# Decode attention: where the spread queries are copied, and the order of turn and values on TensorE

## The chip, the cores and the metric

One NeuronCore of a Trainium2 chip runs the whole program, two decoder layers in one launch. The metric is the time of one execution on the device in microseconds (us); less is better. The engines are TensorE (PE; its weight loads are PEld), VectorE (DVE), ScalarE (ACT), GpSimd (POOL) and SyncE (SP), which only issues transfers. Each engine works its own list of instructions in order, and they meet only at semaphores.

## The reference, cut to what matters

The program computes two layers of a hybrid decoder for a prompt of 1024 tokens and for 8 decode samples of 4 tokens. What the change touches is the attention of the decode samples to their paged cache of 4096 past positions. Each position has 128 latent values and 32 rotary values, which all 8 heads share:

```python
ckv_past = cache_ckv[l][page_table].reshape(DB, past_len, KV_LORA)      # 8 samples x 4096 x 128
kpe_past = cache_kpe[l][page_table].reshape(DB, past_len, ROPE_DIM)     # 8 samples x 4096 x 32
...
s = (jnp.einsum('bthc,blc->bhtl', ql, kc) + jnp.einsum('bthr,blr->bhtl', qp, kr)).astype(jnp.float32) * MLA_SCALE
p = jax.nn.softmax(s, axis=-1).astype(kc.dtype)
return jnp.einsum('bhtl,blc->bthc', p, kc)
```

A sample has 32 query rows (8 heads x 4 tokens). Everything is float32. The same layer holds a gated linear attention (GLA) with a state per sample, whose stage ends just ahead of this one.

## The kernel before, in words

A layer is a row of stages that end in barriers (`stage_end`): every compute engine drains, adds one to `stage_done` and waits for the others. Stage 3 is the GLA; stage 4 is the decode attention, and the change lies in stage 4 and at the end of stage 3.

**Stage 4, one iteration per sample n = 0 to 7.** `cache_load(n)` on GpSimd issues two indirect gathers by page number, of the latent rows (2 MB, into one of four buffers `ck`) and of the rotary rows (0.5 MB, into one of two buffers `kr_c`). DVE turns the keys in five pieces (`turn_keys`, 32x32 block transposes, 128 x 1024): piece 0 is the rotary part, pieces 1 to 4 are 32 latent columns each. The turned piece lies in one of three buffers `ct`. TensorE multiplies each piece with the queries (`scores(n, b)`, 32 matmuls of 64 rows x 256 columns in the records), adding up over the five pieces in PSUM. Then DVE takes the maximum (`maxima`), ACT the exponential (`probs`), TensorE turns the probabilities (`turn_probs`, 8 transposes), ACT copies them to SBUF (`take_probs`), and TensorE multiplies them with the latent rows (`values`, 64 matmuls); ACT keeps the result (`keep_o`). DVE takes the maximum of sample n-1 between its pieces 2 and 3 of sample n.

**The queries.** `q_dec` holds the latent queries with the latent index on the partitions. For piece b, `scores` wants the 32 rows 32(b-1) to 32b of it on all four groups of 32 partitions, since the keys of four groups are turned at a time: `q8[b]`. So `spread_q(b)` copies 32 rows of `q_dec` to four places, and the rest of `q8[b]` is zero. Before the change SP issues these as transfers from SBUF to SBUF: for b = 1, 2 early in stage 3, for b = 3, 4 when `g_zero` is 2. GpSimd gives that mark after two memsets that stand behind `cache_load(1)` in stage 4, and `cache_load(1)` waits until the GLA's states are stored (`states_stored`), because the buffer of gather 1 lies over them. `q8[0]` is written by DVE in stage 2.

**The order on TensorE in stage 4 before the change.** For each n: `scores(n, 0)`, then `values(n-2)` from n = 2 on, then pieces 1 to 3, then `turn_probs(n-1)`, then piece 4. Sample 0 has the scores against the new tokens (`new_scores`) behind its piece 4, 33 matmuls, and DVE takes their maxima (`new_maxima`) before it turns the first keys of sample 1. Gather n waits for the first turned piece of sample n-2 (the rotary buffer is free) and, from n = 4 on, for `pv_done` of sample n-4 (the latent buffer is free).

**At the end of stage 3** DVE makes the operands of the decode samples' GLA (line 2307 gives `g_dve`), TensorE works with them, and the last DVE operations (line 2330) update the eight states. GpSimd has nothing left there after `cache_load(0)`.

**The wait of the change, as it stands in `scores`:**

```python
pe.wait_ge(ct_ready, m + 1)
if n == 0 and b >= 1:
    pe.wait_ge(kr_or_q_moved, 48 + 16 * (8 if b <= 2 else 16))
if b == 0 and n >= 2:
    pe.wait_ge(pd_ready, n)
```

Of the kernel before, what the change touches and what calls it, by code (L numbers as in the profile page):

```python
# [24 lines left out]
P = 128  # L25
DEPTH, D, SEQ, DB, DT = 2, 1024, 1024, 8, 4
KT = D // P
ND = DB * DT
# [5 lines left out]
H, NOPE, ROPE, VD = 8, 64, 32, 64  # L34
# [9 lines left out]
KROW = 32  # L44
BLK = PAST // P
# [14 lines left out]
STEPS = P // KROW + 1  # L60
NCT = 3
# [117 lines left out]
def build(nc, ins, outs):  # L179

    with ExitStack() as ctx:
# [32 lines left out]
        def view(at, *shape):  # L214
            n = int(np.prod(shape))
            v = arena[:, at:at + n]
            names = [f"a{k}" for k in range(len(shape))]
            if len(shape) == 1:
                return v
            return v.rearrange(f"p ({' '.join(names)}) -> p {' '.join(names)}",  # L220
                               **{n_: s for n_, s in zip(names[1:], shape[1:])})
# [37 lines left out]
        q_dec = view(SC, DB, ND)  # L259
        q8 = [view(at, DB, 2, ND) for at in (SC + 2560, SC + 1536, SC + 2048, SC + 4096, SC + 4608)]  # L260
        S2 = SC + 3072
        qswap = [view(S2, TOK), view(SC + 4896, TOK)]
        row_sum, row_rec = view(SC + 1024, 2, 2, NT), view(SC + 1056, 2, 2, NT)
# [28 lines left out]

        ck = [view(at, BLK, P) for at in (XN, XN + 5120, XN + 9216, XN + 13312)]
        kr_c = [view(at, BLK, ROPE) for at in (XN + 4096, XN + 20480)]
        ct = view(XN + 17408, NCT, BLK, KROW)
        pd, pdt = view(SC + 320, 8, P), view(S2, 2, 512)
        o_part = [view(at, P) for at in (SC + 1344, *(SC + 5120 + P * n for n in range(6)), XN + 512)]
        w_sel, o_lat, pn_t = view(XN, DB, ND), view(XN + 256, H, DB, DT), view(XN + 640, 2, ND)
        ckv_rep = view(S2, 4, ND)
        m_all, l_all, m_neg = (view(SC + 256 + DB * k, DB) for k in range(3))  # L300
        m_new, l_new = view(SC + 280, DB), view(SC + 288, DB)
        spare = rope.rearrange("p a n -> p (a n)")
# [206 lines left out]
        def _(sp):  # L509
# [20 lines left out]
            for l in range(DEPTH):  # L530
# [73 lines left out]
                def spread_q(b):  # L604

                    for a in range(4):
                        sp.dma_start(q8[b][KROW * a:KROW * (a + 1), :, a % 2, :], q_dec[KROW * (b - 1):KROW * b]).then_inc(kr_or_q_moved, 16)

# [12 lines left out]
                for h in range(GH):  # L621
                    rows, cols = slice(GK * h, GK * (h + 1)), slice(GV * h, GV * (h + 1))
                    sp.dma_start(outs["gla_s"][bass.ds(l, 1), :, h].rearrange("a b k v -> (a k) b v"), d_state[rows, :, cols]).then_inc(states_stored, 16)
                sp.wait_ge(g_zero, 2)
                for b in (3, 4):
                    spread_q(b)
                sp.wait_ge(stage_done, 4 * (BARRIERS.index(4) + 1))
# [146 lines left out]
        def _(pe):  # L774
# [33 lines left out]
            for l in range(DEPTH):  # L808
# [354 lines left out]
                def new_scores():  # L1163

                    pe.wait_ge(tail_dve, 1)
                    pe.transpose(ps[:, 0, 256:256 + P], ckv_rep.rearrange("p r k -> p (r k)"), ident).then_inc(tail_pe, 1)
                    for n in range(DB):
                        out = ps[0:ND, 0, n * ND:(n + 1) * ND]
                        pe.matmul(out, q_dec[:, n, :], ckv_new, start=True, stop=False)
                        mm = pe.matmul(out, q8[0][64:96, n, 0, :], kr_new[64:96, :], start=False, stop=True)  # L1170
                    mm.then_inc(tail_pe, 1)
# [7 lines left out]
                def scores(n, b):  # L1179

                    m = STEPS * n + b
                    pe.wait_ge(ct_ready, m + 1)
                    if n == 0 and b >= 1:
                        pe.wait_ge(kr_or_q_moved, 48 + 16 * (8 if b <= 2 else 16))
                    if b == 0 and n >= 2:
                        pe.wait_ge(pd_ready, n)
                    for x in range(2):
                        for g in range(4):
                            for h in range(2):
                                r = slice(64 * h, 64 * (h + 1))  # L1190
                                mm = pe.matmul(ps[ND * g:ND * (g + 1), 4 + 2 * (n % 2) + h, 256 * x:256 * (x + 1)], q8[b][r, n, x, :],  # L1191
                                               ct[r, m % NCT, 8 * g:8 * (g + 1), :], start=b + x == 0, stop=b == STEPS - 1, skip_group_check=True)
                    mm.then_inc(sc_done if b == STEPS - 1 else ct_used, 1)
# [24 lines left out]
                for n in range(DB):  # L1218
                    scores(n, 0)
                    if n >= 2:  # L1220
                        values(n - 2)
                    for b in range(1, 4):
                        scores(n, b)
                    if n >= 1:
                        turn_probs(n - 1)
                    scores(n, 4)
                    if n == 0:
                        new_scores()

                values(DB - 2)  # L1230
                pe.wait_ge(tail_dve, 3)
# [751 lines left out]
        def _(dve):  # L1983
# [36 lines left out]
            for l in range(DEPTH):  # L2020
# [125 lines left out]
                def q_pe(i, e):  # L2146

                    h = 2 * i + e
                    dve.wait_ge(q_rope, 4 * i + 1 + e)
                    src = q_h[64:96, 2 * (i % 2) + e, SEQ:TOK].rearrange("p (b t) -> p b t", b=DB)  # L2150
                    for j in range(4):
                        step.mark(dve.tensor_copy(q8[0][32 * j:32 * j + 32, :, j % 2, DT * h:DT * (h + 1)], src))

# [582 lines left out]
        def _(pool):  # L2736
# [29 lines left out]
            for l in range(DEPTH):  # L2766
# [6 lines left out]
                pool.wait_ge(vg_done, NT + 1)  # L2773
                step(pool.memset(q8[0], 0.0))

# [17 lines left out]
                step(pool.memset(d_state, 0.0))  # L2793
                step.mark(pool.memset(q8[1], 0.0))
                step(pool.memset(q8[2], 0.0))
                pool.memset(g_k, 0.0).then_inc(g_zero, 1)
# [22 lines left out]
                def cache_load(n):  # L2819

                    for dst, cache in ((ck[n % NSLOT], "cache_ckv"), (kr_c[n % 2], "cache_kpe")):
                        pool.indirect_dma_start(dst.rearrange("p j c -> p (j c)"), None,
                                                ins[cache].rearrange("l n (q k) c -> (l n q) (k c)", k=KROW),
                                                bass.IndirectOffsetOnAxis(ap=page_i[:, n:n + 1], axis=0)).then_inc(ck_full[n % NSLOT], 16)

                pool.wait_ge(at_done, NT)
                cache_load(0)
                step.restart()
                stage_end(pool, 3)


                for n in range(1, DB):
                    if n == 1:
                        pool.wait_ge(states_stored, 16 * (DB + 4 + 2 * GH))
                    if n >= 2:
                        pool.wait_ge(ct_ready, STEPS * (n - 2) + 1)
                    if n >= NSLOT:
                        pool.wait_ge(pv_done, n - NSLOT + 1)
                    cache_load(n)
                    if n == 1:  # L2840
                        step.mark(pool.memset(q8[3], 0.0))
                        step.sync()
                        pool.memset(q8[4], 0.0).then_inc(g_zero, 1)
                for j in range(NSLOT):
# [190 lines left out]
```

## Time and profile before

| | |
|---|---|
| median of 3 runs | 2570.68 us (2569.37 to 2576.91) |
| the profiled execution | 2552.38 us, span 2550.6 us |
| mean granted TensorE clock of the profiled execution | 0.965 |
| busy: TensorE / weight loads / DVE / ACT / GpSimd | 92% / 54% / 46% / 26% / 19% |
| stage 4, layer one | 516.0 to 636.0 us |
| stage 4, layer two | 1789.2 to 1904.5 us |

The profile is of one execution. The timeline lists runs of instructions of one kind with their start, their length, their line and count, and in brackets the idle time of the engine ahead of them and what ended it; "issue" is a wait for nothing that the profile shows. PE in the windows is TensorE; PEclk is the granted clock, where 1.00 is 2.4 GHz and 0.50 is 1.2 GHz.

### The profile page before, as it was taken

The page shows a single profiled execution, that of the slowest core. Times are in us where ns is not written, and L with a number is a line of the kernel's source. Part 1 is how long each engine was busy: PE and PEld are TensorE (multiplying, and loading weights), DVE is VectorE, ACT ScalarE, POOL GpSimd, SP SyncE. Part 2 cuts the span into 40 slices and gives each one's busy share as a digit, 9 for nine tenths or more (in the row PEclk, how much of TensorE's full clock was granted, in tenths as well). Part 3 has the DMA queues.
Part 4 walks back from the last instruction along what each step waited for, and adds up shares of the span by engine and source line. Part 5 has one row for each costly group of instructions (what it writes and reads, how often), then busy time and mean ns, then how long its engine had stood idle before and what let it go on. Part 6 is the DMA issues. An engine that isn't in the chain of part 4 may idle for free.

```text
span 2550.6 us, 41562 instructions
## 1 busy us (share of the span) xinstructions
PE 2336.2 (92%) x17636; PEld 1385.2 (54%) x17636; DVE 1166.7 (46%) x2074; ACT 653.9 (26%) x1404; POOL 472.5 (19%) x574
## 2 busy tenths in 40 slices
PE   8999998869999999999899999988699999999994
PEld 5645556646666765333366455566466676733332
DVE  2365556855231344333253555568542332633324
ACT  1033444412111331111130334444121022311113
POOL 6003323410100001111260033234100000011113
PEclk9999999978999999999999999999799999999997
DMA  5001001153233128999830010011521421599996
GB/s 190 11 19 30 11 12 42 43 182 119 98 127 120 70 111 323 399 423 423 337 137 11 20 30 11 11 42 43 212 106 55 153 75 66 211 355 409 424 418 255
DMA packets 88224, 391.35 MB, mean 153 GB/s; under 512 B 29390, under 2 KB 33100, under 8 KB 68524
## 3 DMA queue, kind: packets, MB, share of 16 engines
q1 hardware_dynamic: 69884, 309.91, 31.9%
q0 software_dynamic: 17568, 76.57, 7.8%
q8 instruction: 143, 2.34, 0.4%
q10 hardware_dynamic: 576, 2.10, 0.2%
q14 instruction: 53, 0.43, 0.1%
HBM read 355.31 MB, written 41.41 MB: 156 GB/s over the span
## 4 chain that ended last, share of the span: by engine, by line
PE 73%; DVE 11%; issue 4%; ACT 3%; DMA 3%; PEld 2%; POOL 1%; SPq 1%; POOLq 1%; PEldq 0%; DVEq 0%; ACTq 0%
PE ps L1483 12%; PE ps L802 8%; PE ps L825 8%; PE ps L1507 6%; PE ps L1391 5%; PE ps L893 4%; PE ps L973 4%; PE ps L1191 3%; PE ps L985 2%; DVE arena L2224 2%; PE ps L1001 2%; PEld ps L825 2%; PE ps L951 2%; PE ps L1469 2%; DMA arena<-yrow 1%
## 5 line engine op out<-in xcount | busy, mean ns | idle before, releaser
L1483 PE MATMUL ps<-arena 128*32 128x512 f32 x2304 | 317.0, 602 | 21.9 <-issue 16.2
L825 PE MATMUL ps<-arena,ring 128*128 128x352 f32 x936 | 279.9, 462 | 1.0 <-ACTq L487 1.0
L802 PE MATMUL ps<-x,ring 128*128 128x352 f32 x768 | 230.9, 462 | 11.9 <-DMA x<-in_x 10.4
L825 PEld LDWEIGHTS ps<-arena,ring 128*128 128x128 f32 x936 | 178.8, 191 | 100.2 <-issue 1.5
L2655 DVE COPY arena<-ps 128x1024 f32<-128x1024 f32 x44 | 53.9, 1225 | 336.3 <-PE ps L1469 336.3
L802 PEld LDWEIGHTS ps<-x,ring 128*128 128x128 f32 x768 | 146.5, 191 | 93.7 <-issue 13.6
L1483 PEld LDWEIGHTS ps<-arena 128*32 128x32 f32 x2304 | 92.9, 111 | 185.9 <-issue 185.9
L1507 PE MATMUL ps<-arena 128*32 128x512 f32 x1408 | 160.2, 595 | 3.8 <-ACT arena L1900 3.8
L2863 POOL DMA_INDIRECT arena<-xrow,arena x46 | 46.8, 1017 | 590.0 <-DVE arena L2630 319.4
L973 PE MATMUL ps<-arena 96*128 96x512 f32 (+3 forms) x384 | 144.9, 487 | 0.0
L1191 PE MATMUL ps<-arena 64*32 64x256 f32 x2560 | 94.9, 434 | 47.6 <-DMA arena<-arena 31.0
L1391 PE MATMUL ps<-arena,ring 128*128 128x352 f32 x384 | 117.7, 463 | 1.6 <-DVE arena L2488 1.6
L1669 ACT ACTIVATE ring<-ps 128x512 f32<-128x512 f32 (+2 forms) x192 | 87.1, 490 | 120.0 <-PE ps L985 120.0
L893 PE MATMUL ps<-arena,x 128*128 128x512 f32 x256 | 114.6, 608 | 2.2 <-ACT arena L1617 2.2
L1483 PE MATMUL ps<-ring,arena 128*32 128x512 f32 x512 | 116.0, 607 | 0.0
L985 PE MATMUL ps<-consts,ring 128*128 128x128 f32 x576 | 88.5, 280 | 22.2 <-ACT ring L1674 9.1
L1674 ACT ACTIVATE ring<-ps,nmax 128x128 f32<-128x128 f32 (+7 forms) x128 | 94.5, 740 | 52.9 <-DVE nmax L2127 52.4
L2358 DVE STREAM_TRANSPOSE arena<-arena 128x1024 f32<-128x1024 f32 x80 | 95.9, 1227 | 21.5 <-PE ps L1191 17.3
L2125 DVE TENSOR_TENSOR ps<-ps,consts 128x128 f32<-128x128 f32 x128 | 38.3, 299 | 143.8 <-PE ps L973 142.9
L1895 ACT ACTIVATE arena<-ps 128x256 f32<-128x256 f32 x44 | 16.9, 383 | 328.6 <-PE ps L1483 328.6
L2126 DVE TENSOR_REDUCE nmax<-ps 128x1 f32<-128x128 f32 (+7 forms) x128 | 97.0, 758 | 4.4
L1391 PEld LDWEIGHTS ps<-arena,ring 128*128 128x128 f32 x384 | 71.7, 190 | 46.1 <-issue 6.8
(470 smaller groups left out, 3705.1 us busy)
## 6 DMA issues: line engine op xcount, KB each, us to landing
arena<-in_w_gu SPq DMA_DIRECT2D x52, 2048.0 KB, 14.0
arena<-in_w_dn SPq DMA_DIRECT2D x64, 1024.0 KB, 11.9
ring<-in_ring SPq DMA_DIRECT2D x56, 512.0 KB, 3.7
ring<-in_w_gu SPq DMA_DIRECT2D x12, 2048.0 KB, 13.3
arena<-yrow SPq DMA_DIRECT2D x16, 1024.0 KB, 9.4
arena<-in_mem_k SPq DMA_DIRECT2D x16, 512.0 KB, 7.2
arena<-in_mem_v SPq DMA_DIRECT2D x16, 512.0 KB, 9.2
xrow<-arena SPq DMA_DIRECT2D x16, 512.0 KB, 8.6
```

The source lines that it names most:

```text
L802: mm = pe.matmul(ps[:, PIECE_BANKS[n % len(PIECE_BANKS)], 0:CH], ring[:, j % RING, k, :], x[:, k, tok], start=k == 0, stop=k == KT - 1)
L825: mm = pe.matmul(ps[:, (j % 2) * NCH + c, 0:CH], ring[:, j // per, (j % per) * units + k, :], src[:, k, tok], start=k == k0, stop=k == uni ...
L893: mm = pe.matmul(ps[:, 6 + t % 2, :], x[:, k, t * P:t * P + m], wvg[:, k, :], start=k == 0, stop=k == KT - 1)
L973: mm = pe.matmul(ps[:, bank + at // 512, 0:end - at], q_h[0:QK, b, qb * P:(qb + 1) * P], k_h[0:QK, b, at:end], start=True, stop=True)
L985: mm = pe.transpose(ps[:, bank, (kb % 4) * P:(kb % 4 + 1) * P], prob[:, e, kb * P:(kb + 1) * P], ident)
L1191: mm = pe.matmul(ps[ND * g:ND * (g + 1), 4 + 2 * (n % 2) + h, 256 * x:256 * (x + 1)], q8[b][r, n, x, :], ct[r, m % NCT, 8 * g:8 * (g + 1), ...
L1391: mm = pe.matmul(ps[:, (j % 2) * NCH + c, 0:CH], ring[:, slot, (j % 2) * XH + k, :], co[:, k, tok], start=k == 0, stop=k == XH - 1)
L1483: mm = pe.matmul(ps[r, 2 + n % 2, :], xb_t[:, n % 2, k, r], w_gu[e % NW][:, k, :], start=k == 0, stop=k == KT - 1, skip_group_check=True)
L1507: mm = pe.matmul(ps[r, 4 + f, :], h_t[:, k, r], w_dn[e % NW][:, k, f * 512:(f + 1) * 512], start=k == 0, stop=k == 1, skip_group_check=True)
L1674: act.activation(prob[:, e, 0:w], ps[:, 2 * e:2 * e + 2, :].rearrange("p a n -> p (a n)")[:, 0:w], ACT.Exp, bias=nmax[:, e, 1:2], scale=ML ...
L2126: step(dve.reduce_max(nmax[:, e, 0:1], sc, AX))
L2358: dve.transpose(ct[:, m % NCT], keys).then_inc(ct_ready, 1)
```

## The change

The spread queries of pieces 3 and 4 are copied by GpSimd at the end of stage 3, behind `cache_load(0)`, and not by SP; `cache_load(1)` is issued right behind them, ahead of the barrier. For this, buffers are placed anew so that neither the copies nor gather 1 lie over anything that the GLA still needs: `q8` becomes two halves per piece, gather 1's latent buffer moves off the states, and `ct`, `pd`, `o_part`, `ckv_rep` and the maxima move. Gather 2 is now the one that waits for `states_stored`. On TensorE `turn_probs(n-1)` stands behind piece 2 of sample n, and `values(n-1)` behind piece 4. No matmul, no gather and no DVE or ACT operation is added or removed; SP loses eight transfers a layer, and GpSimd gets eight copies.

```diff
-        q8 = [view(at, DB, 2, ND) for at in (SC + 2560, SC + 1536, SC + 2048, SC + 4096, SC + 4608)]
         S2 = SC + 3072
+        Q8 = (SC + 2560, SC + 1536, SC + 2048, S2 + 1280)
+        q8 = [[view(at + DB * ND * x, DB, ND) for x in range(2)] for at in Q8]
+        q8.append([view(at, DB, ND) for at in (S2 + 2592, SC + 1280)])
...
-        ck = [view(at, BLK, P) for at in (XN, XN + 5120, XN + 9216, XN + 13312)]
-        kr_c = [view(at, BLK, ROPE) for at in (XN + 4096, XN + 20480)]
-        ct = view(XN + 17408, NCT, BLK, KROW)
+        ck = [view(at, BLK, P) for at in (XN, XN + 13312, XN + 5120, XN + 9216)]
+        kr_c = [view(at, BLK, ROPE) for at in (XN + 4096, XN + 17408)]
+        ct = view(XN + 18432, NCT, BLK, KROW)
...
 # SP
-                sp.wait_ge(g_zero, 2)
-                for b in (3, 4):
-                    spread_q(b)
...
 # TensorE, scores
-                    if n == 0 and b >= 1:
-                        pe.wait_ge(kr_or_q_moved, 48 + 16 * (8 if b <= 2 else 16))
+                    if n == 0 and b == 1:
+                        pe.wait_ge(kr_or_q_moved, 48 + 16 * 8)
+                    if n == 0 and b == 3:
+                        pe.wait_ge(g_zero, 2)
...
 # TensorE, the loop
                 for n in range(DB):
-                    scores(n, 0)
-                    if n >= 2:
-                        values(n - 2)
-                    for b in range(1, 4):
+                    for b in range(3):
                         scores(n, b)
                     if n >= 1:
                         turn_probs(n - 1)
-                    scores(n, 4)
-                    if n == 0:
+                    for b in range(3, STEPS):
+                        scores(n, b)
+                    if n >= 1:
+                        values(n - 1)
+                    else:
                         new_scores()
 
-                values(DB - 2)
...
 # GpSimd
+                def spread_q(b):
+
+                    for a in range(4):
+                        last = pool.tensor_copy(q8[b][a % 2][KROW * a:KROW * (a + 1)], q_dec[KROW * (b - 1):KROW * b])
+                        if a < 3:
+                            step.mark(last)
+                    return last
+
                 pool.wait_ge(at_done, NT)
                 cache_load(0)
+                pool.wait_ge(g_dve, 1)
+                step.mark(pool.memset(view(Q8[3], 2 * DB, ND), 0.0))
+                step.mark(pool.memset(q8[4][0], 0.0))
+                step(pool.memset(q8[4][1], 0.0))
+                pool.wait_ge(ck_full[0], 32)
+                step.mark(spread_q(3))
+                spread_q(4).then_inc(g_zero, 1)
+                pool.wait_ge(g_zero, 2)
+                cache_load(1)
                 step.restart()
                 stage_end(pool, 3)
 
 
-                for n in range(1, DB):
-                    if n == 1:
+                for n in range(2, DB):
+                    if n == 2:
                         pool.wait_ge(states_stored, 16 * (DB + 4 + 2 * GH))
                     if n >= 2:
                         pool.wait_ge(ct_ready, STEPS * (n - 2) + 1)
                     if n >= NSLOT:
                         pool.wait_ge(pv_done, n - NSLOT + 1)
                     cache_load(n)
-                    if n == 1:
-                        step.mark(pool.memset(q8[3], 0.0))
-                        step.sync()
-                        pool.memset(q8[4], 0.0).then_inc(g_zero, 1)
```

## Rows read from the trace of the kernel before

**Rows 1.** The page: busy times, and the group of line 1191.

```profile
PE 2336.2 (92%) x17636; PEld 1385.2 (54%) x17636; DVE 1166.7 (46%) x2074; ACT 653.9 (26%) x1404; POOL 472.5 (19%) x574
...
L1191 PE MATMUL ps<-arena 64*32 64x256 f32 x2560 | 94.9, 434 | 47.6 <-DMA arena<-arena 31.0
```

**Rows 2.** Timeline of TensorE at the start of stage 4, layers one and two.

```profile
517.42 5.38 PE L1191 MATMUL ps<-arena 64*32 64x256 f32 x96 [2.48 <-DVE arena L2358]
538.33 3.67 PE L1191 MATMUL ps<-arena 64*32 64x256 f32 x64 [15.53 <-DMA arena<-arena]
...
548.21 6.24 PE L1191 MATMUL ps<-arena 64*32 64x256 f32 x128 [2.75 <-DVE arena L2358]
...
1811.51 3.67 PE L1191 MATMUL ps<-arena 64*32 64x256 f32 x64 [15.47 <-DMA arena<-arena]
```

**Rows 3.** Timeline of GpSimd and SP, start of stage 4, layer one.

```profile
519.84 0.94 POOL L2822 DMA_INDIRECT arena<-in_cache_ckv,page_i  x1 [29.86 <-DMA out_gla_s<-arena]
...
523.17 10.71 SPq L607 DMA_DIRECT2D arena<-arena  x8
```

**Rows 4.** GpSimd's groups by line and shape: busy us, mean ns, idle before.

```profile
L2779 POOL TENSOR_TENSOR arena<-arena,rope 32x512 f32<-32x512 f32 x16 | 20.1, 1258 | 1.3 <-DMA arena<-arena 1.3
...
L2859 POOL TENSOR_TENSOR arena<-arena,consts 128x256 f32<-128x256 f32 x8 | 5.8, 724 | 319.3 <-DVE arena L2441 319.3
...
L2843 POOL MEMSET arena<- 128x512 f32 x2 | 1.0, 524 | 0.1
```

**Rows 5.** Timeline of stage 3's end, and line 2822's time from issue to landing.

```profile
489.04 0.95 POOL L2822 DMA_INDIRECT arena<-in_cache_kpe,page_i  x1 [0.30 <-issue]
...
500.66 0.49 DVE L2307 TENSOR_TENSOR arena<-arena 128x128 f32<-128x128 f32 x2
...
DMA to landing us min/median/max: 8.6/9.1/12.4
```

**Rows 6.** Timeline of DVE, first keys of sample 0.

```profile
516.03 4.69 DVE L2358 STREAM_TRANSPOSE arena<-arena 128x1024 f32<-128x1024 f32 x4
```

**Rows 7.** Windows: length, then busy us and count of each engine, PEclk, DMA.

```profile
519.00:520.00 1.00, 1.00 (x27) 0.56 (x19) 1.00 (x2) 0.00 (x0) 0.16 (x1) 0.50 0.00 0
...
523.00:526.00 3.00, 0.00 (x0) 0.00 (x0) 0.00 (x0) 0.00 (x0) 2.02 (x3) 1.00 1.01 421
...
543.20:545.50 2.30, 2.27 (x26) 1.66 (x25) 0.00 (x0) 0.00 (x0) 0.00 (x0) 1.00 0.00 0
```

**Rows 8.** Timeline around the exponentials of sample 2, layer one.

```profile
564.12 1.96 PE L1191 MATMUL ps<-arena 64*32 64x256 f32 x64
566.00 1.50 PE L1213 MATMUL ps<-arena 128*32 128x128 f32 x42
...
565.32 1.25 DVE L2358 STREAM_TRANSPOSE arena<-arena 128x1024 f32<-128x1024 f32 x1 [0.41 <-PE ps L1191]
...
568.91 0.19 ACT L1784 ACTIVATION_READ_ACCUMULATOR arena<-ps,arena 128x1 f32 x1
```

**Rows 9.** Timeline of TensorE in the loop: turns of both layers, a break.

```profile
563.09 1.09 PE L1202 MATMUL ps<-consts,arena 128*128 128x128 f32 x8
...
609.41 1.09 PE L1202 MATMUL ps<-consts,arena 128*128 128x128 f32 x8
...
1835.13 1.09 PE L1202 MATMUL ps<-consts,arena 128*128 128x128 f32 x8
...
1849.29 1.29 PE L1213 MATMUL ps<-arena 128*32 128x128 f32 x37 [0.99 <-issue]
...
1872.25 1.09 PE L1202 MATMUL ps<-consts,arena 128*128 128x128 f32 x8
...
1879.80 1.09 PE L1202 MATMUL ps<-consts,arena 128*128 128x128 f32 x8
```

**Rows 10.** GpSimd beside DVE in stage 3: timeline, and a group of the lines.

```profile
479.26 0.42 DVE L2241 TENSOR_TENSOR arena<-arena 128x256 f32<-128x256 f32 x1
479.35 0.51 POOL L2808 TENSOR_TENSOR arena<-arena 128x64 f32<-128x64 f32 x1 [2.00 <-ACT arena L1716]
...
L2808 POOL TENSOR_TENSOR arena<-arena 128x64 f32<-128x64 f32 x112 | 36.4, 325 | 27.8 <-ACT arena L1716 27.7
```

More of the change, by code:

```diff
@@ L290, in build @@
         d_q0, d_q = view(PR + 192, GH, ND), view(PR + 320, 2, GH, ND)
-        ck = [view(at, BLK, P) for at in (XN, XN + 5120, XN + 9216, XN + 13312)]
-        kr_c = [view(at, BLK, ROPE) for at in (XN + 4096, XN + 20480)]
-        ct = view(XN + 17408, NCT, BLK, KROW)
-        pd, pdt = view(SC + 320, 8, P), view(S2, 2, 512)
-        o_part = [view(at, P) for at in (SC + 1344, *(SC + 5120 + P * n for n in range(6)), XN + 512)]
+        ck = [view(at, BLK, P) for at in (XN, XN + 13312, XN + 5120, XN + 9216)]
+        kr_c = [view(at, BLK, ROPE) for at in (XN + 4096, XN + 17408)]
+        ct = view(XN + 18432, NCT, BLK, KROW)
+        pd, pdt = view(SC + 256, 8, P), view(S2, 2, 512)
+        o_part = [view(at, P) for at in (*(S2 + 1792 + P * n for n in range(6)), XN + 768, XN + 896)]
         w_sel, o_lat, pn_t = view(XN, DB, ND), view(XN + 256, H, DB, DT), view(XN + 640, 2, ND)
-        ckv_rep = view(S2, 4, ND)
-        m_all, l_all, m_neg = (view(SC + 256 + DB * k, DB) for k in range(3))
-        m_new, l_new = view(SC + 280, DB), view(SC + 288, DB)
+        ckv_rep = view(S2 + 1024, 4, ND)
+        m_all, l_all, m_neg = (view(S2 + 1152 + DB * k, DB) for k in range(3))
+        m_new, l_new = view(S2 + 1176, DB), view(S2 + 1184, DB)
         spare = rope.rearrange("p a n -> p (a n)")
@@ L1169, in new_scores @@
                         pe.matmul(out, q_dec[:, n, :], ckv_new, start=True, stop=False)
-                        mm = pe.matmul(out, q8[0][64:96, n, 0, :], kr_new[64:96, :], start=False, stop=True)
+                        mm = pe.matmul(out, q8[0][0][64:96, n, :], kr_new[64:96, :], start=False, stop=True)
                     mm.then_inc(tail_pe, 1)
@@ L1190, in scores @@
                                 r = slice(64 * h, 64 * (h + 1))
-                                mm = pe.matmul(ps[ND * g:ND * (g + 1), 4 + 2 * (n % 2) + h, 256 * x:256 * (x + 1)], q8[b][r, n, x, :],
+                                mm = pe.matmul(ps[ND * g:ND * (g + 1), 4 + 2 * (n % 2) + h, 256 * x:256 * (x + 1)], q8[b][x][r, n, :],
                                                ct[r, m % NCT, 8 * g:8 * (g + 1), :], start=b + x == 0, stop=b == STEPS - 1, skip_group_check=True)
@@ L2151, in q_pe @@
                     for j in range(4):
[L2152 removed]
+                        step.mark(dve.tensor_copy(q8[0][j % 2][32 * j:32 * j + 32, :, DT * h:DT * (h + 1)], src))
                 def inverse(i, hf):
@@ L2773, in _ @@
                 pool.wait_ge(vg_done, NT + 1)
-                step(pool.memset(q8[0], 0.0))
+                step(pool.memset(view(Q8[0], 2 * DB, ND), 0.0))
                 def rope_q(h, hf, cols):
@@ L2793, in _ @@
                 step(pool.memset(d_state, 0.0))
-                step.mark(pool.memset(q8[1], 0.0))
-                step(pool.memset(q8[2], 0.0))
+                step(pool.memset(view(Q8[1], 4 * DB, ND), 0.0))
                 pool.memset(g_k, 0.0).then_inc(g_zero, 1)
```

2 lines of the change are left out of this document (1 added, 1 removed).

## The prediction

> **What bounds the kernel now.** I read the page first, then the PE rows of the timeline in the decode attention stage, then what DVE, SP and GpSimd did in the same stretch, and last the clock windows. The page [rows 1] shows TensorE busy for 92% of the span, so only time in which TensorE stands still, or runs at the lower clock, is worth anything. One of its lines speaks of this change: the scores of line 1191 were held for 47.6 us, and 31.0 of it ended with a transfer from SBUF to SBUF.
>
> The timeline says where [rows 2]. In each layer TensorE does the first three score pieces of sample 0, stands for 15.5 us, does the other two and the new scores, stands 2.75 us, and goes into the loop over samples 1 to 7. The 15.5 us are the copies of the spread queries for pieces 3 and 4: SP issues eight transfers one after the other from 523.17, which takes 10.71 us, and the last lands at 538.3 [rows 3]. SP waited there for two memsets of GpSimd, which stood behind the issue of gather 1, and that behind a wait of 29.86 us for the stores of the states. 2 x 15.5 is the 31.0 of the page.
>
> **The spread copies.** What goes: eight SP transfers and the wait for them. What comes: before the barrier that ends the gated-linear stage GpSimd does three memsets (512, 256 and 256 columns), eight copies of 32 partitions x 256, and the two issues of gather 1. The trace has no copy of that form, nor any GpSimd operation that reads one group of partitions and writes another. The nearest rows [rows 4]: a memset of 512 columns takes 0.52 us, so 0.27 us for 256 is the lower end; a two-input operation on 128 x 256 takes 0.72, and on 32 x 512 1.26 us, the upper end. A copy reads one tensor and writes one, so I take 0.45, between the memset and the two-input operation of its width. Eight are 2.2 to 10.1 us, taken as 3.6.
>
> When: the copies wait for g_dve, which DVE's last multiply at line 2307 gives at 501.15, and for gather 0, whose second half was issued at 489.04 and with the longest landing of 12.4 us is there by 501.4 [rows 5]. Memsets from 501.2 to 502.3, copies to 505.9 (504.5 to 512.4), gather 1 issued in 2.5 us (twice 0.94 [rows 3] and two gaps of 0.3), so GpSimd is done at 508.4 (507.0 to 514.9). The barrier falls when DVE ends, just ahead of its first key transpose at 516.0 [rows 6]. GpSimd was idle all this time; even the upper end is hidden by 1 us. If that cover is gone, every us more of GpSimd is a us more per layer.
>
> With the queries there, piece 3 needs only its turned keys, and DVE had turned them at 520.7 (four transposes from 516.03 in 4.69 us [rows 6]). So it starts when piece 2 ends, at 522.8. **15.5 us less per layer.**
>
> **What this wait's end does to the clock.** The windows [rows 7] show the granted clock at 0.50, TensorE's lower level of 1.2 GHz, while the first pieces run, and at 1.00 in 523 to 526, right after 5.4 us of scores, when TensorE had nothing to do; then it fell again in the idle time. The clock was full again only from 543.2. From the start of piece 3 to the end of the new scores it took 7.1 us (538.33 to 548.21 less 2.75 [rows 2]). At the full clock two pieces take 1.88 (564.12 to 566.00 in [rows 8]), and 26 matmuls of the new scores took 2.27 us [rows 7], so that its 33 take 2.9. With no idle time ahead of them all this falls into the raised clock: 7.1 us become 4.8, **2.3 less per layer**. Bounds: 0 (the clock stays low) and 2.3. After that come the same 2.75 us of idle time as before (new maxima on DVE, then the first keys), since DVE's order is not changed.
>
> **The order in the loop.** Now turn follows piece 2, and values of sample n-1 close the iteration. A clean iteration takes 7.55 us from turn to turn (1872.25 to 1879.80 [rows 9]): turn 1.03, two pieces 1.88 (563.09 to 564.12 to 566.00), values as long, 1.89, and three pieces 2.75. The new order does the same work. The question is what is late at the new places. Turn waits for the exponentials of the sample before. DVE starts the transpose of piece 2 at 565.32, when the last piece has freed the keys' buffer at 565.1; it then takes the maximum, and ACT is through with exp at 569.1 [rows 8]. That is 4.0 us, 4.2 with the slip of 0.2 that DVE gets where it waits for piece 3 to free a buffer. TensorE comes to turn 1.89 + 2.75 = 4.64 us after the last piece: **0.4 us to spare, no wait** in the steady loop. In the first iteration no values lie in front: the first four pieces took 6.2 us at DVE's pace [rows 2], and the exponentials of sample 0, with ACT's table load, were there only when they ended. Piece 3 covered part of that and now stands behind it: **0.9 more per layer**, one piece. In iteration 7 the end is as before: values of sample 6 behind the last piece.
>
> Gathers 4 to 7 wait for the values of three samples before. Before: issue of its first half and landing 1.2 + 9.1 = 10.3 us [rows 3, 5], one transpose 1.2, one piece 0.9, values 1.9, for two iterations: 7.2 us each. After: 10.3, three transposes 3.5, maximum and exp 2.6, turn 1.0, two pieces 1.9, values 1.9, for three: 7.1 each. Both are below TensorE's 7.55, so a gather doesn't set the pace unless it lands late (at 12.4, 8.8 before and 8.2 after). What does cost: five iterations (turn 1 to turn 6) took 46.3 us in layer one and 44.7 in layer two [rows 9], 8.6 and 6.9 more than clean. Much of it is breaks of 1 to 2 us in the middle of a run of one kind ("issue"), as the 0.99 before the last 37 matmuls of values, while gathers are under way. The change removes no matmul and no gather, so I leave them: **0**, with 0 to 15.5 for both layers as the bound of a gain.
>
> **Small costs.** Gather 2 now runs (519.8 to 530) while TensorE works at pieces 3 and 4 and the new scores, and a break as above may fall there: 0 to 1.5, taken as 0.5. GpSimd's copies run beside the DVE operations that end the stage. A GpSimd operation of 64 columns took 0.51 us when it met DVE's at line 2241, and 0.32 is the mean of its line [rows 10]. Two such DVE operations fall beside the copies and are on the way to the barrier: 0 to 0.7 each, a whole copy of the upper width, taken as 0.4 together. The Trainium skill (SBUF — State Buffer, "SBUF: two separate sides") speaks against this part: it says that a DVE operation with two SBUF inputs and a GpSimd operation that reads SBUF can't run together, and whichever comes second waits for all of the other. By that rule both DVE operations could wait for a whole copy, 0.9 us instead of my 0.4, and the sum would be 1 us less gain; the trace agrees in so far as the GpSimd operation stretches.
>
> **Sum.** Per layer -15.5 - 2.3 + 0.9 + 0.5 + 0.4 = -16.0, twice -32.0. The profiled execution (2552.4 us) becomes 2520.4. It was 18 us under the median of the timed runs (2570.7); the terms are waits in this stage and don't hang on that, so I take them off the median: **2539 us**.
>
> **Rivals.**
> A, more comes than the terms: gathers start earlier by one piece (0.9 us) and the loop loses its late landings and breaks. For it: the five iterations took longer in layer one than in layer two for the same work, so something of it is not fixed. Against: a break in the middle of values waits for no gather of its own. Half of the 15.5 us or more: 2524 to 2531. Chance 0.16.
> B, turn waits for exp. For it: 0.4 us is thin, and 1.6 us are missing if DVE is not ahead of TensorE when piece 2 ends (maximum and exp 2.6 after its transpose, less the piece). Seven iterations in two layers at 0.5 to 1.6: 7 to 22 us back, 2546 to 2561. Against: the values of 1.89 us are what lets DVE get ahead. Chance 0.17.
> C, slower: GpSimd holds the barrier. Place: the eight copies from quadrant to quadrant, the one operation without a row. They are hidden up to (515.8 - 2.5 - 502.3) / 8 = 1.4 us each; all gain of 16 us a layer is gone at 3.4 us each, and at 5 us each the kernel is 25 us slower, 2596. Against: a two-input operation of twice the columns on 32 partitions takes 1.26 us [rows 4]. Chance 0.03.
> D, no change: the wait goes into another. Piece 3 is free, but gather 1 or 2 is late: it would have to come 16 us after it is needed; gather 1 lands at about 517 (507 and 9.1), and DVE wants it at 529. Chance 0.03.
>
> **How the numbers follow.** My forecast has 0.61, with 2533 to 2546 of its own: port and breaks at either end, the clock term taken or not (5 us). A and B lie on both sides of it; the range reaches through most of A and to two thirds of B: 2524 to 2555. About 0.3% (8 us) is what a measurement of this kernel can tell from no change. Faster takes the forecast, A and nearly all of B: 0.93; same 0.035; slower 0.035.
>
> **What the profile would show.** The line 1191 group without a release by a transfer from SBUF to SBUF, and 160 score matmuls of sample 0 in one piece, ending at about 524.7 with the clock up from 522.6. The first score of sample 1 some 17 us earlier, at 531. GpSimd's copies between 502 and 506, 0.45 us each, and the last DVE operation of the stage still at 515.8 (if later: the port, or C). Turn (line 1202) with no idle time before it except in sample 1. Five iterations in 44 to 47 us. The prediction is wrong if turn waits each time, if a break opens in sample 0's scores, or if the time of the stage's end shows less than 28 us saved over both layers.

## The result, and the profile after

| | before | changed | ratio, 95% interval |
|---|---|---|---|
| first timing | 2572.9 us | 2528.2 us (2524.5 to 2534.2) | 0.9828 [0.9803, 0.9854] |
| second, another job | 2568.8 us | 2533.0 us (2527.2 to 2536.0) | 0.9856 [0.9833, 0.9879] |
| third, another job | 2560.8 us | 2531.8 us (2523.3 to 2534.6) | 0.9869 [0.9847, 0.9891] |

In a job both kernels are timed side by side. The change makes the kernel faster, by 45, 36 and 29 us in the three, and no interval reaches 1. The forecast was 2539 us, 32 less (ratio 0.988), with 2524 to 2555 as its range.

The profiled execution of the changed kernel took 2527.99 us (span 2526.2), against 2552.38 of before. These two differ by 24 us only: the profiled execution of before was a short one. So the stage is compared by itself, and further down with a second profile of before.

The page of the changed kernel, the group of the score matmuls (answers to [rows 1]; the line is now 1192):

```profile
PE 2333.4 (92%) x17636; PEld 1382.3 (55%) x17636; DVE 1170.5 (46%) x2074; ACT 654.1 (26%) x1404; POOL 481.1 (19%) x590
...
L1192 PE MATMUL ps<-arena 64*32 64x256 f32 x2560 | 90.5, 419 | 19.4 <-DVE arena L2358 12.9
```

The transfer is gone as a releaser, and of 47.6 us of idle time ahead of the scores 19.4 are left. The timeline of TensorE at the start of stage 4, layer one and layer two (answers to [rows 2]):

```profile
519.74 6.46 PE L1192 MATMUL ps<-arena 64*32 64x256 f32 x160 [3.91 <-DVE arena L2358]
...
532.02 5.38 PE L1192 MATMUL ps<-arena 64*32 64x256 f32 x96 [2.74 <-DVE arena L2358]
538.15 1.09 PE L1203 MATMUL ps<-consts,arena 128*128 128x128 f32 x8 [0.75 <-ACT arena L1784]
...
1778.83 6.67 PE L1192 MATMUL ps<-arena 64*32 64x256 f32 x160 [3.53 <-DVE arena L2358]
```

All five pieces of sample 0 run in one piece, 160 matmuls. But the wait ahead of them is 3.91 us, where it was 2.48. Two timelines of the changed kernel say why. DVE's at the end of stage 3:

```profile
515.40 1.25 DVE L2330 SCALAR_TENSOR_TENSOR arena<-arena,ps 128x256 f32<-128x256 f32 x3
518.22 0.23 DVE L2338 COPY arena<-arena 128x128 f32<-128x128 f32 x1 [1.57 <-POOLq L489]
```

GpSimd's over the same stretch:

```profile
501.94 0.52 POOL L2836 MEMSET arena<- 128x512 f32 x1 [11.22 <-DVE arena L2307]
...
503.03 4.79 POOL L2828 COPY arena<-arena 32x256 f32<-32x256 f32 x8
...
509.37 0.94 POOL L2821 DMA_INDIRECT arena<-in_cache_kpe,page_i  x1 [0.30 <-issue]
```

DVE is done at 516.65 and goes on at 518.22, released by GpSimd's queue. GpSimd had issued its last instruction at 509.4 to 510.3. What it was at until 518.2 the timeline does not say; the landing time of the gather does: 8.6 us after 509.37 are 518.0. In layer two it is 8.3 us after 1768.80, that is 1777.1, and DVE goes on at 1777.30.

Where the stage's time went, from the two profiles, per layer (start to start, from the timelines; "sample 0" leaves the 15.5 us out):

| stretch | before | changed | difference |
|---|---|---|---|
| wait for the spread queries | 15.53 / 15.47 | 0 | -15.5 / -15.5 |
| line 2307 to the stage's first DVE operation (2338) | 15.2 / 15.2 | 16.8 / 16.5 | +1.6 / +1.3 |
| sample 0, first score to end of new scores | 12.5 / 12.5 | 9.5 / 9.7 | -3.0 / -2.8 |
| samples 1 to 7, first score to end of values(6) | 65.1 / 62.3 | 63.8 / 64.1 | -1.4 / +1.7 |
| the stage's tail | 22.3 / 20.4 | 21.3 / 21.4 | -1.0 / +1.0 |
| sum | | | -19.3 / -14.2 |

That is 33.4 us for both layers, where the sum of the prediction had 32.0.

### The profile page after: what moved, and what is told of

Read it like the earlier page. It is cut to its first block, busy times and chain, and to the rows that moved or that the text cites. A ratio compares the mean times of both kernels' runs of the same rounds, so it can differ in the third digit from the quotient of the medians.

```text
span 2526.2 us, 41560 instructions
## 1 busy us (share of the span) xinstructions
PE 2333.4 (92%) x17636; PEld 1382.3 (55%) x17636; DVE 1170.5 (46%) x2074; ACT 654.1 (26%) x1404; POOL 481.1 (19%) x590
## 4 chain that ended last, share of the span: by engine, by line
PE 74%; DVE 11%; issue 5%; ACT 3%; PEld 3%; DMA 2%; POOL 1%; POOLq 1%; PEldq 1%; SPq 0%; ACTq 0%; DVEq 0%
PE ps L1483 12%; PE ps L801 9%; PE ps L824 8%; PE ps L1507 6%; PE ps L1391 5%; PE ps L892 4%; PE ps L972 4%; PE ps L1192 3%; PE ps L984 2%; PE ps L1000 2%; PEld ps L824 2%; DVE arena L2224 2%; PE ps L950 2%; PE ps L1469 2%; PE ps L1214 1%
## 5 line engine op out<-in xcount | busy, mean ns | idle before, releaser
L801 PE MATMUL ps<-x,ring 128*128 128x352 f32 x768 | 231.1, 463 | 12.5 <-DMA x<-in_x 11.1
L1192 PE MATMUL ps<-arena 64*32 64x256 f32 x2560 | 90.5, 419 | 19.4 <-DVE arena L2358 12.9
```

The costliest lines, as they stand in the source:

```text
L801: mm = pe.matmul(ps[:, PIECE_BANKS[n % len(PIECE_BANKS)], 0:CH], ring[:, j % RING, k, :], x[:, k, tok], start=k == 0, stop=k == KT - 1)
```

## The experiments

For each run I also give the length of the stage with the end of the one ahead of it: from ScalarE's exponential of the decode samples' GLA (`g_eb[0][:, 0:ND]`) to ScalarE's last copy of stage 4 (`mix[:, 2:6, SEQ:TOK]`), both layers added. In the first profiles it is 268.6 before and 235.2 after. "Five iterations" is the time from turn 1 to turn 6, given for layer one and layer two.

**The kernel before, profiled again (c0).** No edit.

> The kernel before, unchanged, profiled again. The timed runs put the change at -44.7 us, the two profiles at -24.4. If the first profile of before was simply a short execution, this one has a span near 2570 and the added us lie outside the decode attention stage, in the expert stage with its weight transfers. If the wait of 15.5 us per layer is longer in most executions (a rival for the larger gain), it shows here as more than 31.0 us by a transfer from SBUF to SBUF.

Measured: span 2567.2, stage 276.4. The waits by the transfer are 14.77 and 15.06 us, not longer than in the first profile. So the rival (a longer wait in most executions) has nothing for it here. Of the 16.6 us by which this execution is longer, 7.8 lie in the stage, and most of these in the loop: from turn 0 to turn 6 it takes 57.3 and 56.7 us where it took 55.0 and 52.3 (the five iterations 47.6 and 47.1, where they took 46.3 and 44.7). I had expected all of it outside.

**The changed kernel, again, beside it (c1).** No edit.

> The changed kernel, unchanged: the control for the others of this job. Ratio 0.980 to 0.985 to the kernel before. In its trace GpSimd should again hold the barrier ahead of the decode stage until gather 1 has landed: the first DVE operation of the stage (line 2338) 1.2 to 1.6 us later than DVE's own end, with GpSimd's queue as the releaser.

Measured: 0.9856 [0.9833, 0.9879], span 2531.9, stage 243.6, five iterations 46.7 and 48.1. Against the profile of before of the same job the stage is 32.8 us shorter, of 35.3 us in all. GpSimd's queue held the barrier in both layers, by 1.59 and 1.77 us. The second of these and the ratio lie just outside what I gave.

**One half alone (e1): the spread copies, TensorE's old order.**

```diff
                 for n in range(DB):
-                    for b in range(3):
+                    scores(n, 0)
+                    if n >= 2:
+                        values(n - 2)
+                    for b in range(1, 4):
                         scores(n, b)
                     if n >= 1:
                         turn_probs(n - 1)
...
+                values(DB - 2)
```

> Spread copies and the early gather kept, TensorE's order as before. My sum (the spread is all, the new order costs 0.9 us per layer in the first iteration): 1 to 3 us faster than the changed kernel, no wait of turn for the exponentials in sample 1 (0.75 us each now). Rival A (the new order frees the loop): 5 to 15 us slower than the changed kernel, with five iterations (turn 1 to turn 6) at 46 us or more against the 45.3 and 45.6 us of the changed kernel.

Measured: 2531.3 us, ratio 0.9856 [0.9831, 0.9882], the changed kernel's own in that job (2533.0, 0.9856); stage 246.4, five iterations 49.8 and 47.2. Turn had no wait in sample 1, as I had said. The five iterations of over 46 us are one of rival A's marks, but the changed kernel of the same job has 46.7 and 48.1, and the other mark, 5 us or more on the time, did not come. The spread copies alone give all of the gain that can be measured.

**The other half alone (e2): the new order in the kernel before.** The edit is the reverse, in the kernel before.

> TensorE's new order alone in the kernel before. My sum: the same as before to 3 us slower, the wait of 15.5 us per layer still there. Rival A: 5 to 15 us faster than before.

Measured: 1.0025 [1.0007, 1.0043], 2 to 11 us slower; stage 276.7 beside the 276.4 of before. The new order by itself brings nothing and costs some us, by the medians 7, where I had given 3 at most. Turn waited 0.82 and 1.00 us for the exponentials in sample 1; where the rest went is not shown. Both runs speak against rival A's cause, gathers that start one piece earlier.

**Who holds the barrier (e4): gather 1 behind it.**

```diff
                 pool.wait_ge(g_zero, 2)
-                cache_load(1)
                 step.restart()
                 stage_end(pool, 3)
+                cache_load(1)
```

> Gather 1 issued behind the barrier of stage 3, GpSimd's copies still ahead of it. Theory: GpSimd's drain lasts until gather 1 has landed (issue of its second half at 509.37 and 8.6 us of landing are 518.0, and the barrier fell at 518.2), so here the first DVE operation of the stage follows DVE's own end by 0.1 to 0.2 us and not by 1.2 to 1.9 us. Rival: the eight copies themselves make the drain long; then the gap stays over 1 us. Gather 1 then lands some 11 us after the barrier, when DVE wants it, so sample 1 may start up to 1 us late: stage time within 2 us of the changed kernel.

DVE's timeline of this run:

```profile
514.44 1.24 DVE L2330 SCALAR_TENSOR_TENSOR arena<-arena,ps 128x256 f32<-128x256 f32 x3
515.82 0.23 DVE L2338 COPY arena<-arena 128x128 f32<-128x128 f32 x1
```

The gap is 0.14 us with the eight copies still there. So it is not the copies: the drain of GpSimd ahead of the barrier lasts as long as a gather that it has issued is on its way. The 1.5 us went elsewhere, though (one execution: 2530.5 us, stage 243.0). The scores of sample 0 took 8.2 us, with a break of 0.43 in them, and 7.7, for the 6.5 and 6.7 of the changed kernel. Two windows rows, the changed kernel's and then this run's, each from 4.2 to 5.2 us after the first score of layer one:

```profile
523.94:524.94 1.00, 1.00 (x49) 0.73 (x41) 0.81 (x1) 0.00 (x0) 0.00 (x0) 1.00 0.94 393
```

```profile
521.54:522.54 1.00, 1.00 (x32) 0.61 (x24) 0.81 (x1) 0.00 (x0) 0.00 (x0) 0.50 0.98 416
```

In the changed kernel the granted clock fell some 2.9 and 2.4 us ahead of the first score and was back at 1.00 some 4.0 and 4.4 us after it. Here, where TensorE stood for 2.47 us and not for 3.91 and 3.53, it fell 1.4 and 1.3 us ahead and was back 5.4 and 5.5 us after. Gather 1, which now ran beside the scores, is not needed for this: in e9 further down gather 1 has landed before, and the clock is back as late (5.0 to 5.5 us, scores of 7.0 to 7.2 us). From DVE's end to the last score it is 9.6 and 9.4 us in the changed kernel and 8.7 to 8.9 in the two runs of e9, so about half of the 1.4 and 1.1 us that the barrier costs comes back through the clock.

**Gather 1 ahead of the copies, and ScalarE copies (e5).** GpSimd issues gather 1 first, and ScalarE, which idles there, does the copies; TensorE's wait ahead of piece 3 becomes `g_zero` 3:

```diff
 # ScalarE
                 take_kt(NT, ND)
+                act.wait_ge(g_zero, 2)
+                for b in (3, 4):
+                    for j in range(4):
+                        last = act.activation(q8[b][j % 2][KROW * j:KROW * (j + 1)], q_dec[KROW * (b - 1):KROW * b], ACT.Copy)
...
 # GpSimd
-                step(pool.memset(q8[4][1], 0.0))
-                pool.wait_ge(ck_full[0], 32)
-                step.mark(spread_q(3))
-                spread_q(4).then_inc(g_zero, 1)
-                pool.wait_ge(g_zero, 2)
+                step.sync()
+                pool.memset(q8[4][1], 0.0).then_inc(g_zero, 1)
                 cache_load(1)
```

> GpSimd issues gather 1 right behind its memsets, and ScalarE does the eight copies in its idle time (6.4 us) at the end of stage 3. Theory: gather 1 lands by 514.5, DVE ends at 516.6, so the gap ahead of the first DVE operation of the stage is 0.1 to 0.2 us, as before the change, 1.2 to 1.5 us less per layer. Rival: any gather in flight near the barrier costs; then the gap is over 0.5 us here too. Eight ScalarE copies take 0.3 to 0.4 us each, hidden.

Measured: gap 0.13 and 0.14 us, stage 232.4, one execution of 2528.0 us. The copies on ScalarE's timeline:

```profile
505.10 3.47 ACT L1775 ACTIVATE arena<-arena 32x256 f32<-32x256 f32 x8
```

One every 0.43 us, hidden in its idle time, against 0.60 on the average of GpSimd's eight.

**What slows the loop (e6): no gathers for samples 4 to 7.**

```diff
                     if n >= NSLOT:
-                        pool.wait_ge(pv_done, n - NSLOT + 1)
+                        continue
                     cache_load(n)
```

> The changed kernel without the gathers of samples 4 to 7: these samples use the cached rows of samples 0 to 3 again, so that part of the computation is changed. Theory: the breaks and slow stretches of TensorE in the loop (issue) come from its instructions arriving late while a gather starts or runs, so five iterations (turn 1 to turn 6) come down from 45 to 48 us to 38 to 40 us, 7.55 to 8 each, with breaks left only in the first two. Rival: they belong to the instruction stream alone; then the five iterations stay at 44 us or more. A second rival, gathers landing late, would show as waits of DVE for a transfer, which the changed kernel's trace does not have.

The waits that count landed gathers are cut to match. Measured: one execution of 2503.0 us, stage 219.2. First the windows row of the changed kernel over its five iterations of layer one, then the same of this run (columns as in [rows 7]):

```profile
545.69:590.99 45.30, 40.31 (x1169) 27.95 (x1161) 36.09 (x36) 12.30 (x25) 6.18 (x8) 1.00 0.60 231
```

```profile
544.15:581.88 37.73, 37.73 (x1169) 27.52 (x1161) 35.65 (x36) 12.30 (x25) 0.25 (x1) 1.00 0.02 4
```

TensorE's timeline of this run, one iteration:

```profile
559.24 1.09 PE L1203 MATMUL ps<-consts,arena 128*128 128x128 f32 x8
560.26 1.96 PE L1192 MATMUL ps<-arena 64*32 64x256 f32 x64
562.15 1.96 PE L1214 MATMUL ps<-arena 128*32 128x128 f32 x64
564.03 2.82 PE L1192 MATMUL ps<-arena 64*32 64x256 f32 x96
566.79 1.09 PE L1203 MATMUL ps<-consts,arena 128*128 128x128 f32 x8
```

7.55 us from turn to turn, five times in a row, TensorE busy for all of it at the full clock. With the gathers it has the same 1169 matmuls and 45.3 us. So the loop's 7 to 12 us per layer over its clean time belong to the gathers; the run takes their issue and their traffic away together. They are no waits for a gather's data. DVE's timeline of the changed kernel has none for a transfer in the loop of layer one and one in layer two, 0.73 us at 1814.34, behind which TensorE had no wait. The breaks carry "issue", as here in its layer one:

```profile
564.86 1.93 PE L1192 MATMUL ps<-arena 64*32 64x256 f32 x57
569.07 0.63 PE L1192 MATMUL ps<-arena 64*32 64x256 f32 x7 [2.28 <-issue]
```

One wait for keys covers all 32 matmuls of a piece, so nothing in the program can stop TensorE seven matmuls ahead of a piece's end. That its instructions come late is what is left; the page counts 144 packets of instructions on one queue and 53 on another, and the Trainium skill (Runtime: NRT & Kernel Launch, "Instruction fetch mechanics") says that each engine's sequencer fetches its next page by DMA while it executes the current one. No run here separates this from another effect of the gathers.

A long break costs more than itself, since the clock falls behind it. In layer two of the changed kernel TensorE stood for 2.17 us, and the 96 scores after it took 4.38 us instead of 2.82, the first of them at a granted clock of 0.50:

```profile
1820.54 0.46 PE L1214 MATMUL ps<-arena 128*32 128x128 f32 x2 [2.17 <-issue]
1820.93 4.38 PE L1192 MATMUL ps<-arena 64*32 64x256 f32 x96
```

**A kernel that takes both leftovers (e9): e5, and the new maxima later.** DVE takes the maxima of the new tokens behind the maximum of sample 0, in the middle of sample 1:

```diff
                         if b == 3 and n >= 1:
                             maxima(n - 1)
+                            if n == 1:
+                                new_maxima()
                         turn_keys(n, b)
-                    if n == 0:
-                        new_maxima()
```

> As e5, and DVE takes the maxima of the new tokens behind the maximum of sample 0, in the middle of sample 1, and not ahead of its keys. Theory: TensorE's 2.75 us of idle time ahead of sample 1 go, since its keys are turned while it does the new scores, and 1.3 us per layer at the barrier: together about 4 us per layer, 8 us less than the changed kernel. Rival: the wait only moves to turn in sample 1 (the exponentials come 6.1 us after the first score because DVE and ACT do them one after the other, with the new maxima now behind the maximum of sample 0): then 3 to 5 us in all.

Measured: 2515.9 us, 0.9802 [0.9781, 0.9823], stage 227.1. Again, beside the changed kernel (c2 for the changed kernel, then e9):

> The changed kernel, the control of this job: ratio 0.980 to 0.988 to the kernel before. Five iterations (turn 1 to turn 6) between 45 and 48 us in each layer, the first DVE operation of the decode stage held 1.2 to 2 us by GpSimd's queue.

Measured: 2531.8 us, 0.9869 [0.9847, 0.9891], stage 243.2, barrier held by 1.35 and 1.49 us. Of the five iterations two are a little off what I gave: 49.1 us in layer one (turns at 546.41 and 595.48) and 49.4 in layer two.

> ScalarE's copies, the early gather 1 and the later new maxima once more, beside the changed kernel on one chip. The first timing of it and the control before it were of two jobs (ratios 0.9802 and 0.9856). Theory (the barrier's 1.5 us and the 2.75 us ahead of sample 1, per layer): 6 to 10 us less than the changed kernel. Rival (the difference was between the jobs): 0 to 4 us less.

Measured: 2520.6 us, 0.9844 [0.9819, 0.9869], stage 228.5. The medians are 11 us apart, the intervals overlap. The stage is 15 us shorter than the changed kernel's of the same job, more than the 6 to 10 that I gave; 3 of the 15 lie in the five iterations, which scatter by as much without any edit. TensorE's timeline of this run:

```profile
521.46 7.18 PE L1192 MATMUL ps<-arena 64*32 64x256 f32 x160 [2.47 <-DVE arena L2365]
...
531.65 2.99 PE L1192 MATMUL ps<-arena 64*32 64x256 f32 x96
534.57 1.09 PE L1203 MATMUL ps<-consts,arena 128*128 128x128 f32 x8
```

The wait ahead of sample 1 is gone, and turn came 2.9 us after the first score of sample 1 and not 6.1. The rival (the wait only moves to turn) falls.

**The clock by itself (e10).** e9 with matmuls that nobody reads, ahead of line 1131 and at the start of the stage:

```diff
-                keep_clock(5, 16)
+                keep_clock(5, 40)
                 pe.wait_ge(g_dve, 1)
...
+                keep_clock(1, 24)
                 for n in range(DB):
```

> e9 with matmuls that nobody reads: 24 more ahead of the decode samples' part of stage 3, where TensorE idles 2.9 us, and 24 at the start of the decode stage. It tests the clock term (2.3 us per layer in the prediction) by itself. Theory: the clock falls to 0.50 because of the idle time ahead, so with it filled the 16 matmuls of line 1141 take 3.5 to 5 us and not 6.2, and the scores of sample 0 run at DVE's pace (six us and not 7.2) or the clock is full when they begin: 2 to 4 us less per layer, 4 to 8 in all. Rival: the clock falls for another reason or the added matmuls start late and hold the scores: no gain, up to 3 us per layer lost.

Measured: 2527.6 us, 0.9856 [0.9833, 0.9880], stage 231.7, against 228.5 of e9 in that job. TensorE's timeline:

```profile
506.48 3.61 PE L1141 MATMUL ps<-arena 128*32 128x256 f32 x16 [0.41 <-DVE arena L2324]
...
515.77 7.85 PE L777 MATMUL ps<-consts 128*128 128x128 f32 x48 [0.79 <-DVEq L489]
523.55 4.73 PE L1192 MATMUL ps<-arena 64*32 64x256 f32 x160
```

The clock answers as said: line 1141 takes 3.61 us and not 6.15, and 160 score matmuls 4.73 us and not 7.2. But the fillers were far too many. The 48 records at the lower clock held the scores by 6 us, and the gain was eaten. My expectation had the clock's answer and not the price of the filler. Cut to fit (e11):

```diff
-                keep_clock(5, 40)
+                keep_clock(5, 28)
...
-                keep_clock(1, 24)
+                keep_clock(1, 7)
```

> As e10, with the unread matmuls cut to the idle time that they fill: 12 ahead of line 1131 and not 24 (each is two in the records, and 24 ran 2.6 us too long), 7 at the start of the decode stage and not 24 (those ran 7.8 us at the lower clock and held the scores by 6 us). Theory: line 1141 again takes 3.6 us and not 6.2, with line 1131 starting no later than in e9, and the scores of sample 0 end 1 to 2 us sooner after the barrier: 7 to 9 us less than e9 in both layers' stages together, where e10 gave 4 back. Rival: the shorter filling leaves the clock at 0.50; then the stages are within 2 us of e9's 227 and 228 us.

Two windows rows, of e9 (second run) and of this run, over the 16 matmuls of line 1141:

```profile
508.10:514.10 6.00, 6.00 (x16) 2.40 (x16) 1.21 (x1) 4.07 (x11) 0.61 (x1) 0.57 1.00 369
```

```profile
508.60:512.10 3.50, 3.50 (x17) 1.60 (x17) 1.21 (x1) 3.33 (x9) 0.55 (x1) 1.00 1.02 360
```

Granted clock 0.57 there and 1.00 here. Stage 223.6: 3.5 and 4.9 us less than the two runs of e9, not the 7 to 9 that I gave. The end of stage 3 has its 2.2 to 2.6 us per layer; of the second filler nothing is left: the scores of sample 0 took 6.0 and 5.9 us, but then the clock was low again in the first scores of sample 1, which took 4.5 us for 2.9. No idle time stood ahead of this fall. Two windows rows of this run, over the new scores and over the first scores of sample 1:

```profile
527.10:530.40 3.30, 3.30 (x51) 2.46 (x57) 3.30 (x3) 0.00 (x0) 1.87 (x2) 1.00 0.96 406
531.00:533.50 2.50, 2.50 (x58) 1.60 (x48) 2.40 (x5) 2.49 (x4) 0.00 (x0) 0.50 1.11 472
```

TensorE had been at work without a break since 517.81, the last 3 us of it with the small matmuls of the new scores. So idle time is one thing behind which the clock falls here, and not the only one. The time, 2523.7 us with 0.9860 [0.9831, 0.9889], doesn't tell it from e9. So e9 is the version that the runs support as faster than the changed kernel by its stage (6.7 to 16.5 us shorter in every pairing of profiles; the medians of one job are 11 us apart, with intervals that overlap), and e11 has the shortest stage in one profile.

## Why the prediction was right, point by point

**The wait and where it goes.** Right. 15.5 us per layer are gone, and e1 shows that the spread copies alone do it.

**GpSimd's copies.** Taken as 3.6 us, measured 4.79 for the eight, inside the bounds. They started at 503.0 (502.3 predicted), in a timeline that is 0.7 us later. By itself a copy was sized right: five of the eight took 0.39 to 0.40 us, and one followed the other every 0.45. The 1.2 us more are the port, below.

**The cover at the barrier.** The step that failed is "GpSimd is done at 508.4 ... The barrier falls when DVE ends". GpSimd's last issue ended at 510.3, but its drain lasted until gather 1 had landed at 518.0. I had costed the issue of the gather and not its landing, though rival D has the landing "at about 517", behind the barrier, as a question of the data alone. Price: +1.4 and +1.1 us per layer, against 0 in the sum. e4 and e5, where the gap is 0.13 to 0.14 us, show the cause.

**The port.** Taken at 0.4 per layer: line 2307 to DVE's last end is 15.10 and 15.01 us before and 15.27 and 15.30 after, 0.2 to 0.3. One operation of line 2242 took 0.50 and not 0.42, one of line 2322 1.34 and not 1.21. The sum has only DVE's side of it; GpSimd waited more. The changed kernel's timelines of DVE and of GpSimd:

```profile
505.75 1.34 DVE L2322 TENSOR_TENSOR arena<-arena,consts 32x1024 f32<-32x1024 f32 x1 [0.96 <-ACT arena L1728]
```

```profile
506.08 1.28 POOL L2828 COPY arena<-arena 32x256 f32<-32x256 f32 x1
```

This copy took 1.28 us instead of 0.39 and ended 0.27 us after DVE's operation at 507.09. The first two copies, beside lines 2241 and 2242, took 0.65 and 0.48. That fits the rule that I had taken as speaking against my 0.4 (the Trainium skill, SBUF — State Buffer, "SBUF: two separate sides"): the one that comes second waits for what is left of the other, here a short piece of a copy for DVE and 0.9 us of line 2322 for GpSimd. GpSimd had the time to spare, so it cost nothing.

**Clock and breaks in sample 0.** -2.3 + 0.5 = -1.8 predicted, -3.0 and -2.8 measured. No break fell there in this profile, and the clock was full from about 523.7, 4 us after the scores began, where the prediction had it 5.2 us after. That is the barrier again: held longer, TensorE's clock fell earlier and came back earlier, and in e4 and e9, without the hold, it was back only 5.0 to 5.5 us after the first score. So the two misses hang together. e10 and e11 show that the fall of the clock in the 2.9 us gap ahead of line 1131 comes with TensorE's idle time there; what else makes it fall stays open, since it also fell in e11 without any.

**The loop.** The 0.9 us of the first iteration are there (turn at 538.15 with 0.75 us of wait for ACT, 6.13 us after the first score). In the later iterations turn has no wait: 0.4 us to spare was enough, and rival B did not come. Leaving the breaks at 0 was right on average (-1.4 and +1.7 with these 0.9, so -2.3 and +0.8 without), and for a reason that the prediction did not have: they move with each execution. Five iterations took 44.7 to 49.8 us in the profiles of one and the same work.

**The sum.** 32.0 us predicted for the stage, 33.4 and 32.8 measured in two pairs of profiles. That it fits to 1.4 us is in part luck: the barrier cost 2.5 us that the sum does not have, and sample 0 gave 2.2 us more than its terms. Of the signs of being wrong that the prediction names, none came in this profile. The times say 29 to 45, so the forecast of 2539 is 11 us above the first median. The pair of profiles of one job leaves 2.5 us outside the stage. The first timing's gain of 45 us is 9 more than these 35.3, and its interval (38 to 51 us) doesn't reach down to them; the rest stays open.

**Rivals.** A would have given the first median (2528), but its cause is not there: e1, without the new order, is as fast, and e2 has no gain. B did not come; C and D did not either.

## What to carry to other kernels

When a copy is moved to an engine that idles ahead of a barrier, count what that engine has in flight at the barrier, not only its last instruction: a gather issued 6 us ahead of it held all engines by over a us, of which part came back only because TensorE's clock then rose sooner in the scores. An engine that is busy for 92% of the span still had 15.5 us in one place that one row names, and that row's idle time was worth its face value. A reordering that looks free by the arithmetic of one iteration is to be tried alone: here it gave nothing, and without the copies the kernel was 2 to 11 us slower with it.

## What the runs showed of the hardware

- GpSimd's drain ahead of a barrier ended with the landing of its gather (issue of the second half at 509.37, 8.6 us of landing, barrier passed at 518.2); without a gather in flight the gap was 0.13 to 0.14 us.
- TensorE lost 7 to 12 us in five iterations that take 37.7, with no semaphore to wait for, while 201 to 234 GB/s were moved on average; with 4 GB/s it lost none. The granted clock over these stretches was 1.00 in most, 0.93 to 0.97 in those with the long breaks.
- TensorE's clock came back sooner after the first score where it had fallen sooner ahead of it: 4.0 and 4.4 us after it behind waits of 3.91 and 3.53 us (changed kernel), 5.0 to 5.5 us after it behind waits of 2.47 us (e4, both runs of e9).
- Unread matmuls in 2.9 us of idle time held the granted clock of the next stretch at 1.00, where it had been 0.57, and cut 16 matmuls of 128x256 from 6.15 to 3.61 us; 48 records of filler at the lower clock cost 7.85 us. In e11 the clock fell to 0.50 with no idle time for 13 us ahead.
- A copy of 32 partitions x 256 columns to other partitions took 0.39 us on GpSimd and 0.41 on ScalarE. Beside a DVE operation with two inputs in SBUF one of GpSimd's took 1.28 us, and ended 0.27 us after that operation.
